# The delta rule's triangular inverse on compact 32x32 diagonal blocks, built by products with its transpose, in place of full 128x128 tiles

## The chip, the cores and the metric

The kernel runs on one NeuronCore of a Trainium2 chip. The metric is the device time of one execution in microseconds (us).

## The reference, cut to what matters

The program is two blocks of two layers each on 256 tokens of width 1024, in fp32: a gated convolution beside a gated DeltaNet, an HGRN2 layer, then a conformer convolution and an attention layer with their MLPs. The change lies in the DeltaNet of the first layer, which has 8 heads of 128 columns. Per head and chunk, with gc the running sum of the gates:

```python
low = jnp.where(strict, jnp.einsum("bhnid,bhnjd->bhnij", kb, k) * decay, 0.0)
rhs = jnp.concatenate([v * beta, kb * jnp.exp(gc)[..., None]], axis=-1)
sol = lax.linalg.triangular_solve(low + jnp.eye(c, dtype=jnp.float32), rhs,
                                  left_side=True, lower=True, unit_diagonal=True)
```

The solution gives the new values of the chunk; with them the state and the outputs are computed. The reference takes chunks of 64 tokens; the kernel takes 128, which is the same function, so that it has two chunks and inverts 128x128 unit triangular matrices.

## The kernel before, in words

Activations lie transposed, 128 channels on the partitions and 256 tokens in a row. A large product is done in halves (`half`, lines 409 to 411): weights are split into a high part (ScalarE, line 542) and a low part (VectorE, line 555) and each of 8 blocks takes three products of 128x128 by 256 columns, 24 instructions. SyncE's queue brings the weights in units of 1 MB into three buffers; some units hold rows of another matrix that VectorE reduces beside the rest (line 547). The order on each engine is written out by hand and engines meet at semaphores.

In the DeltaNet stage the eight heads are two groups of four (g = 0, 1), a matrix of each head in one quarter of a PSUM bank; each group has three banks b0, b1, b2. `weave` runs the groups' generators in turn, a step of group 0, a step of group 1, then one step of the filler: on TensorE one half product of the gated convolution, the output projection or the z gate (`pe_fill`). ScalarE and VectorE have the same order (`ac_group`, `ve_group`, with `ac_fill`, `ve_fill`).

For each chunk c (two), `pe_group` writes the differences of the gates (line 693, a product with 8 rows), k by k and q by k products (lines 698, 702). VectorE forms the decayed matrix DD (line 296, ScalarE takes the exponential at line 1213), LT = DD times k by k (L1848) and its first masked part ML (L1850), AT_ (L1852) and YY = identity less ML (L1854). TensorE transposes ML (line 300, the helper `tr`) and VectorE makes XX of it (L1860) and the next mask (L1862). Then come six levels s = 1 to 6 (LEVELS is 7); XX is the inverse of the diagonal blocks of size 2^s, YY its transpose. A level has two steps with a filler between:

```python
t = pe.matmul(PS[b0][:, blk(m)], ML[:, m, :], XX[:, m, :], start=True, stop=True)
...
t = pe.matmul(PS[b1][:, blk(m)], YY[:, m, :], PP[:, m, :], start=True, stop=True)
```

The first step (line 730) multiplies the masked off-diagonal part by XX; from level 2 on, four transposes of XX (line 300) into b2 stand ahead of it and ScalarE copies them to YY (L1226). ScalarE copies the product to PP (L1228), the second step (line 742) multiplies by YY, and VectorE subtracts it from XX (L1875); it makes the next ML beside (L1871). Level 6 forms the transpose alone (line 746, L1877). With YY the stage goes on to the new values (line 758), the outputs and the state (lines 765, 769). The convolution of the third layer (`pe_taps`, line 929) has products of 32x32 tiles, and `pe_level` (line 865) and `pe_tap_sum` (line 938) other small ones.

GpSimd clears a few buffers and issues side transfers in order (`pool_program`). The constants K come in one transfer: identity, ones, masks `gm` of seven levels, and `quad`, an identity of 32 repeated down the partitions.

## Time and profile before

| what | us |
|---|---|
| median of 3 runs (1408.59 to 1410.61) | 1410.13 |
| the profiled execution | 1410.44 |
| its span | 1408.3 |
| TensorE busy, share of the span | 1348.1, 96% |
| weight loads busy | 1248.9, 89% |
| VectorE busy | 975.4, 69% |
| ScalarE busy | 747.4, 53% |
| GpSimd busy | 22.4, 2% |

The profiled execution is one run of the program; the span goes from its first to its last instruction, and 2.1 us of the run's time lie around it. Busy times are sums over the whole span. A TensorE instruction is recorded from its start to the end of its pipeline, so that successive ones overlap in the record, and the distance of their starts tells what each takes. Line numbers, as L742, are those of the kernel; a helper has one line for all of its callers.

### The profile page before, as it was taken

Reading aid. Unit: us, or ns where it says so; the run is one execution under the profiler, and the core shown is the slowest. Engines: PE = TensorE matmul, PEld = TensorE weight load, DVE = VectorE, ACT = ScalarE, POOL = GpSimd, SP = SyncE. Lnnn points to the kernel's source line nnn. Section 1 sums busy time; section 2 is a strip of 40 time slices with the busy share of each in tenths; the row PEclk is TensorE's granted clock in tenths of the full one; section 3 lists DMA queues with packets and bytes.
Section 4 is the critical chain, followed back from the end, with each engine's and each line's share of the span. In section 5 each row is a group of like instructions: output and inputs, shape, how many; then the busy total and the mean of one; then the engine's idle time right before and its main releaser. Section 6 shows DMA issues by size and latency. Waiting matters only on the chain.

```text
span 1408.3 us, 24667 instructions
## 1 busy us (share of the span) xinstructions
PE 1348.1 (96%) x10464; PEld 1248.9 (89%) x10464; DVE 975.4 (69%) x1491; ACT 747.4 (53%) x989; POOL 22.4 (2%) x53
## 2 busy tenths in 40 slices
PE   6998998999989999999799998899999999999998
PEld 5997998999979999999798776888888998988887
DVE  4887977765466788777644686788776676576543
ACT  6666344437454455555245413778634686487531
POOL 0000000000000000000000000000000000000000
PEclk9998999999999999999899999999999999999999
DMA  6555553444266555555232323568875433355551
GB/s 254 184 194 191 183 215 133 188 168 147 98 224 225 182 202 190 205 209 181 91 120 90 121 91 122 180 222 288 300 269 206 150 120 121 131 185 194 190 195 64
DMA packets 34637, 247.22 MB, mean 176 GB/s; under 512 B 3872, under 2 KB 3872, under 8 KB 4960
## 3 DMA queue, kind: packets, MB, share of 16 engines
q1 hardware_dynamic: 29968, 213.40, 42.2%
q0 software_dynamic: 4560, 32.25, 6.5%
q8 instruction: 83, 1.36, 0.4%
q14 instruction: 26, 0.21, 0.0%
HBM read 244.58 MB, written 1.05 MB: 174 GB/s over the span
## 4 chain that ended last, share of the span: by engine, by line
PE 82%; DVE 8%; ACT 6%; issue 3%; DMA 1%; DVEq 0%; ACTq 0%
PE PS L467 14%; PE PS L409 9%; PE PS L410 9%; PE PS L411 9%; PE PS L468 7%; PE PS L482 6%; PE PS L865 3%; ACT WH L542 3%; DVE WL L555 2%; PE PS L425 2%; PE PS L929 2%; PE PS L426 2%; PE PS L427 2%; PE PS L742 1%; PE PS L730 1%
## 5 line engine op out<-in xcount | busy, mean ns | idle before, releaser
L555 DVE TENSOR_TENSOR WL<-RAW,WH 128x2048 fp32r<-128x2048 f32 x166 | 380.0, 2289 | 118.3 <-ACT WH L542 115.0
L542 ACT ACTIVATE WH<-RAW 128x2048 fp32r<-128x2048 f32 x166 | 317.0, 1910 | 182.2 <-PE PS L468 71.2
L409 PE MATMUL PS<-XW,WH 128*128 128x256 f32 x1024 | 301.1, 294 | 16.8 <-DVE WL L555 12.4
L410 PE MATMUL PS<-XW,WH 128*128 128x256 f32 x1024 | 293.2, 286 | 0.0
L411 PE MATMUL PS<-XW,WL 128*128 128x256 f32 x1024 | 292.9, 286 | 0.0
L409 PEld LDWEIGHTS PS<-XW,WH 128*128 128x128 f32 x1024 | 200.0, 195 | 18.4 <-DVE WL L555 12.4
L410 PEld LDWEIGHTS PS<-XW,WH 128*128 128x128 f32 x1024 | 200.1, 195 | 0.2
L411 PEld LDWEIGHTS PS<-XW,WL 128*128 128x128 f32 x1024 | 199.8, 195 | 0.0
L467 PE MATMUL PS<-XW,WH 128*128 128x512 f32 x392 | 141.0, 398 | 0.2
L296 DVE SCALAR_TENSOR_TENSOR BIG<-BIG,C 128x256 f32<-128x256 f32 (+2 forms) x228 | 101.4, 505 | 30.0 <-ACT BIG L1264 13.5
L468 PE MATMUL PS<-XW,WL 128*128 128x256 f32 x392 | 109.9, 280 | 0.0
L482 PE MATMUL PS<-BIG,RAW 128*128 128x258 f32 (+1 forms) x448 | 102.9, 387 | 2.2 <-issue 2.2
L482 PEld LDWEIGHTS PS<-BIG,RAW 128*128 128x128 f32 x448 | 85.2, 192 | 18.8 <-issue 6.7
L467 PE MATMUL PS<-YW,WH 128*128 128x512 f32 x256 | 90.7, 398 | 0.0
L467 PEld LDWEIGHTS PS<-XW,WH 128*128 128x128 f32 x392 | 73.7, 188 | 16.5 <-DVE WL L555 0.9
L467 PE MATMUL PS<-HX,WH 128*128 128x512 f32 x240 | 85.4, 397 | 0.0
L468 PEld LDWEIGHTS PS<-XW,WL 128*128 128x128 f32 x392 | 74.0, 189 | 2.3
L468 PE MATMUL PS<-YW,WL 128*128 128x256 f32 x256 | 71.9, 281 | 0.0
L547 DVE CUSTOM_DVE_ANT_0 BIG<-BIG,CB 128x1024 f32<-128x1024 f32 x60 | 71.2, 1224 | 0.0
L468 PE MATMUL PS<-HX,WL 128*128 128x256 f32 x240 | 67.5, 281 | 0.0
L409 PE MATMUL PS<-YW,WH 128*128 128x256 f32 x224 | 67.1, 299 | 0.2 <-DVE YW L1788 0.2
L410 PE MATMUL PS<-YW,WH 128*128 128x256 f32 x224 | 65.4, 292 | 0.0
(368 smaller groups left out, 2677.4 us busy)
## 6 DMA issues: line engine op xcount, KB each, us to landing
RAW<-wst SPq DMA_DIRECT2D x200, 1024.0 KB, 4.9
BIG<-wad POOLq DMA_DIRECT2D x30, 1024.0 KB, 5.1
X<-xT SPq DMA_DIRECT2D x1, 1024.0 KB, 4.9
outT<-X SPq DMA_DIRECT2D x4, 256.0 KB, 4.2
K<-cst SPq DMA_DIRECT2D x1, 656.0 KB
CB<-crow SPq DMA_DIRECT2D x1, 512.0 KB
BIG<-pT POOLq DMA_DIRECT2D x2, 256.0 KB, 4.2
C<-cols SPq DMA_DIRECT2D x1, 370.0 KB
```

What stands on the lines that cost most here:

```text
L296: return ve.scalar_tensor_tensor(out=o, in0=a, scalar=s, in1=b, op0=op0, op1=op1)
L409: pe.matmul(o, h, hl[0][:, k0 + k, :], start=(k == 0), stop=False)
L410: pe.matmul(o, h, hl[1][:, k0 + k, :], start=False, stop=False)
L411: t = pe.matmul(o, l, hl[0][:, k0 + k, :], start=False, stop=(k == 7))
L425: pe.matmul(o, h, wh[:, k, :], start=(k == 0), stop=False)
L467: pe.matmul(two(b + n), h, op, start=start, stop=False)
L468: return pe.matmul(PS[b + n][:, 0:T], l, op[:, 0, :], start=False, stop=False)
L482: t = pe.matmul(o, w[:, k, n * 128:(n + 1) * 128], op(k), start=(k == 0), stop=(k == 7))
L542: ac.activation(WH[p % NS][:, :], RAW[u % NR][:, :], ACT.Copy).then_inc(S.hi.tick(p), 1)
L547: t = ve.tensor_tensor_reduce(out=w, in0=w, in1=CB1[:, :], scale=1.0, scalar=0.0, op0=ALU.mult, op1=ALU.add, accum_out=MOD[:, 2 * n + m:2 ...
L555: ve.tensor_tensor(WL[p % NS][:, :], RAW[u % NR][:, :], WH[p % NS][:, :].bitcast(f32), ALU.subtract).then_inc(S.lo.tick(p), 1)
L865: t = pe.matmul(PS[b][:, m * 64:(m + 1) * 64], k[:, m // 2, blk(m % 2)], qs[:, m, :, 1, :], start=True, stop=True)
```

## The change

The inverse of the four diagonal blocks of 32 is kept compact: for each head 128 partitions by 32 columns, block a on partitions 32a to 32a+31. XYB holds X in its first four heads' columns and Y, the transpose, in the other four.

- VectorE makes LTB, the diagonal blocks of LT, in four operations on 32 partitions each, masks them with `gmb` (MLB) and starts Y from `quad`; the first transpose becomes a product of MLB by `quad`.
- Levels 1 to 4: TensorE takes each product as 16 matmuls of 32x32 by 32 columns for a group. It forms both X's and Y's update, 32 matmuls, from the same copy PPB, and VectorE subtracts both in one operation of 128x256. The transposes of XX and the copies to YY go.
- Level 5 joins pairs of blocks: 8 matmuls with LT, then 12, for X and Y. ScalarE copies Y's diagonal blocks into YY (four operations) and writes the negated off-diagonal ones (two); VectorE writes XG, the part of X that level 6 needs.
- Level 6: for each head one matmul with 64 rows and one with 32, then one of 64x64; VectorE writes the last quarter of YY.
- YY is cleared once by GpSimd, one memset per group. The constants lose two masks of 128 columns and gain `gmb` of 160.

The diff, with lines of context and some plain ones left out:

```diff
-CST = [("ident", 128), ("ones", 128), ("neg", 128), ("gm", 896), ("quad", 32)]
+CST = [("ident", 128), ("ones", 128), ("neg", 128), ("gm", 640), ("quad", 32), ("gmb", 160)]
...
+    put("gmb", np.concatenate([np.concatenate([v[32 * c:32 * c + 32, 32 * c:32 * c + 32] for c in range(4)]) for v in lv], 1).astype(np.float32))
...
+        LTB = [view(7168 + 4096 * g, 4, 32) for g in range(2)]
+        MLB = [view(7296 + 4096 * g, 4, 32) for g in range(2)]
+        XYB = [view(7680 + 4096 * g, 8, 32) for g in range(2)]
+        PPB = [view(6144 + 4096 * g, 4, 32) for g in range(2)]
+        XG = [view(6272 + 4096 * g, 4, 32) for g in range(2)]
+        PP6 = [view(6400 + 4096 * g, 4, 64) for g in range(2)]
...
+            for g in range(2):
+                gp.wait_ge(*S.l2.ve(g, 1))
+                gp.memset(CHB[g][4], 0.0).then_inc(S.gdn.gp.tick("zero", g), 1)
...
-                    t = tr(pe, PS[b0][:, blk(m)], ML[:, m, :])
+                    for a in range(4):
+                        r = slice(32 * a, 32 * a + 32)
+                        t = pe.matmul(PS[b0][r, 32 * m:32 * m + 32], MLB[g][r, m, :], K[r, CST0["quad"][0]:CST0["quad"][0] + 32], start=True, stop=True)
...
-                        vacate(pe, b2, "yy", g, c, s)
-                        for m in range(4):
-                            t = tr(pe, PS[b2][:, blk(m)], XX[:, m, :])
-                        t.then_inc(S.gdn.pe.tick("yy", g, c, s), 1)
...
-                    pe.wait_ge(*S.gdn.ve("ml", g, c, s))
+                    pe.wait_ge(*(S.gdn.ve("ml", g, c, s) if s < 5 else S.bank[b1]("kk", g, c)))
...
-                        t = pe.matmul(PS[b0][:, blk(m)], ML[:, m, :], XX[:, m, :], start=True, stop=True)
+                        if s < 5:
+                            for a in range(4):
+                                r = slice(32 * a, 32 * a + 32)
+                                t = pe.matmul(PS[b0][r, 32 * m:32 * m + 32], MLB[g][r, m, :], XB[r, m, :], start=True, stop=True)
+                        elif s == 5:
+                            for a in (0, 64):
+                                r, o = slice(a, a + 32), slice(a + 32, a + 64)
+                                t = pe.matmul(PS[b0][o, 32 * m:32 * m + 32], LT[r, m, o], XB[r, m, :], start=True, stop=True)
+                        else:
+                            pe.matmul(PS[b0][64:128, 64 * m:64 * m + 32], LT[0:64, m, 64:128], XG[g][0:64, m, :], start=True, stop=True)
+                            t = pe.matmul(PS[b0][64:128, 64 * m + 32:64 * m + 64], LT[32:64, m, 64:128], XB[32:64, m, :], start=True, stop=True)
...
-                    if s < 6:
+                    if s < 5:
...
                         for m in range(4):
-                            t = pe.matmul(PS[b1][:, blk(m)], YY[:, m, :], PP[:, m, :], start=True, stop=True)
+                            for a in range(4):
+                                r = slice(32 * a, 32 * a + 32)
+                                pe.matmul(PS[b1][r, 32 * m:32 * m + 32], YB[r, m, :], PPB[g][r, m, :], start=True, stop=True)
+                        for m in range(4):
+                            for a in range(4):
...
+                                t = pe.matmul(PS[b1][r, 128 + 32 * m:160 + 32 * m], PPB[g][r, m, :], YB[r, m, :], start=True, stop=True)
+                    elif s == 5:
...
+                        for m in range(4):
+                            pe.matmul(PS[b1][32:64, 32 * m:32 * m + 32], YB[32:64, m, :], PPB[g][32:64, m, :], start=True, stop=True)
+                            for a in (0, 64):
...
+                                t = pe.matmul(PS[b1][r, 128 + 32 * m:160 + 32 * m], PPB[g][o, m, :], YB[o, m, :], start=True, stop=True)
...
+                        pe.wait_ge(*S.gdn.ac("y5", g, c))
...
                         for m in range(4):
-                            t = pe.matmul(PS[b2][:, blk(m)], PP[:, m, :], YY[:, m, :], start=True, stop=True)
+                            t = pe.matmul(PS[b2][0:64, 64 * m:64 * m + 64], PP6[g][64:128, m, :], YY[64:128, m, 64:128], start=True, stop=True)
...
+                    if s == 6:
+                        ac.wait_ge(*S.gdn.pe("p", g, c, 5))
+                        for a in (64, 0):
+                            t = ac.activation(YY[a:a + 32, :, a + 32:a + 64], PS[b1][a:a + 32, 128:256].rearrange("p (a b) -> p a b", a=4), ACT.Copy, scale=-1.0)
+                        t.then_inc(S.gdn.ac.tick("y5", g, c), 1)
...
-                    if s > 1:
-                        ac.wait_ge(*S.gdn.pe("yy", g, c, s))
-                        ac.activation(YY, grp(b2), ACT.Copy).then_inc(S.bank[b2].tick("yy", g, c, s, on="ac"), 1)
...
-                    ac.activation(PP, grp(b0), ACT.Copy).then_inc(S.bank[b0].tick("pp", g, c, s, on="ac"), 1)
+                    if s < 6:
+                        ac.activation(PPB[g], PS[b0][:, 0:128].rearrange("p (a b) -> p a b", a=4), ACT.Copy).then_inc(S.bank[b0].tick("pp", g, c, s, on="ac"), 1)
+                    else:
+                        ac.activation(PP6[g][64:128, :, :], PS[b0][64:128, 0:256].rearrange("p (a b) -> p a b", a=4), ACT.Copy).then_inc(S.bank[b0].tick("pp", g, c, s, on="ac"), 1)
+                    if s == 5:
+                        ac.wait_ge(*S.bank[b1]("xx", g, c, 4))
+                        if c == 0:
+                            ac.wait_ge(*S.gdn.gp("zero", g))
+                        for a in range(0, 128, 32):
+                            ac.activation(YY[a:a + 32, :, a:a + 32], YB[a:a + 32, :, :], ACT.Copy)
...
+                for a in range(0, 128, 32):
+                    t = ve.tensor_tensor(LTB[g][a:a + 32, :, :], DD[a:a + 32, :, a:a + 32], grp(b1)[a:a + 32, :, a:a + 32], ALU.mult)
+                t.then_inc(S.gdn.ve.tick("ltb", g, c), 1)
+                ve.wait_ge(*own("ve"))
+                ve.tensor_tensor(MLB[g], LTB[g], bm(cs("gmb", 0, 32), 4), ALU.mult).then_inc(S.gdn.ve.tick("ml", g, c, 0), 1)
+                ve.wait_ge(*own("ve"))
+                ve.tensor_tensor(YB, bm(cs("quad", 0, 32), 4), MLB[g], ALU.subtract).then_inc(S.gdn.ve.tick("y0", g, c), 1)
                 ve.tensor_tensor(LT, DD, grp(b1), ALU.mult).then_inc(S.bank[b1].tick("kk", g, c, on="ve"), 1)
-                ve.wait_ge(*own("ve"))
-                ve.tensor_tensor(ML, LT, bm(cs("gm"), 4), ALU.mult).then_inc(S.gdn.ve.tick("ml", g, c, 0), 1)
...
-                ve.wait_ge(*S.gdn.ve("ml", g, c, 0))
-                ve.tensor_tensor(YY, bm(cs("ident"), 4), ML, ALU.subtract).then_inc(S.gdn.ve.tick("y0", g, c), 1)
...
-                ve.tensor_tensor(XX, bm(cs("ident"), 4), grp(b0), ALU.subtract).then_inc(S.bank[b0].tick("x0", g, c, on="ve"), 1)
+                ve.tensor_tensor(XB, bm(cs("quad", 0, 32), 4), small(PS[b0][:, 0:128]), ALU.subtract).then_inc(S.bank[b0].tick("x0", g, c, on="ve"), 1)
...
-                    if s < 6:
+                    if s < 4:
                         ve.wait_ge(*S.gdn.pe("m", g, c, s))
-                        ve.tensor_tensor(ML, LT, bm(cs("gm", 128 * s + 128), 4), ALU.mult).then_inc(S.gdn.ve.tick("ml", g, c, s + 1), 1)
+                        ve.tensor_tensor(MLB[g], LTB[g], bm(cs("gmb", 32 * s + 32, 32), 4), ALU.mult).then_inc(S.gdn.ve.tick("ml", g, c, s + 1), 1)
+                    if s == 5:
+                        ve.wait_ge(*S.bank[b1]("xx", g, c, 4))
+                        ve.tensor_copy(XG[g][0:32, :, :], XB[0:32, :, :])
...
-                    if s < 6:
-                        ve.tensor_tensor(XX, XX, grp(b1), ALU.subtract).then_inc(S.bank[b1].tick("xx", g, c, s, on="ve"), 1)
+                    if s < 5:
+                        ve.tensor_tensor(XYB[g], XYB[g], small(PS[b1][:, 0:256]), ALU.subtract).then_inc(S.bank[b1].tick("xx", g, c, s, on="ve"), 1)
+                    elif s == 5:
+                        ve.wait_ge(*S.gdn.ac("y5", g, c))
+                        ve.tensor_scalar(XG[g][32:64, :, :], small(PS[b1][32:64, 0:128]), -1.0, None, ALU.mult).then_inc(S.bank[b1].tick("xx", g, c, s, on="ve"), 1)
                     else:
-                        ve.tensor_tensor(YY, YY, grp(b2), ALU.subtract).then_inc(S.bank[b2].tick("yq", g, c, on="ve"), 1)
+                        ve.tensor_scalar(YY[0:64, :, 64:128], PS[b2][0:64, 0:256].rearrange("p (a b) -> p a b", a=4), -1.0, None, ALU.mult).then_inc(S.bank[b2].tick("yq", g, c, on="ve"), 1)
```

## Rows read from the trace of the kernel before

**Rows 1.** The page, busy time by engine: us, share, instructions

```profile
PE 1348.1 (96%) x10464; PEld 1248.9 (89%) x10464; DVE 975.4 (69%) x1491; ACT 747.4 (53%) x989; POOL 22.4 (2%) x53
```

**Rows 2.** Stretches of 20 us: busy TensorE, weight loads, VectorE, ScalarE, GpSimd, clock

```profile
130.00:150.00 20.00, 16.24 (x100) 15.54 (x99) 17.33 (x35) 7.98 (x11) 0.00 (x0) 0.75 0.23 82
150.00:170.00 20.00, 20.00 (x172) 19.83 (x173) 16.95 (x26) 6.69 (x11) 0.00 (x0) 1.00 0.58 212
...
230.00:250.00 20.00, 14.16 (x95) 13.53 (x94) 19.09 (x31) 4.49 (x6) 0.00 (x0) 0.83 0.28 106
...
sum 200.00, PE 184.87 PEld 181.11 DVE 155.78 ACT 88.22 POOL 0.00; mean PE 18.49 PEld 18.11 DVE 15.58 ACT 8.82 POOL 0.00
```

**Rows 3.** The chain, 157 to 171 us: start, length, engine, tile, line

```profile
164.28 1.78 PE PS L742 x16
...
168.46 0.12 PE PS L411
...
168.94 0.44 PE PS L300 x4
169.38 0.89 PE PS L730 x8
```

**Rows 4.** TensorE's waits, 130 to 305 us: total, times, longest

```profile
PE PS L300 <- DVE BIG L1850: 7.5, 2, 4.4
PE PS L742 <- ACT BIG L1228: 2.6, 2, 1.5
PE PS L730 <- DVE BIG L1862: 2.0, 2, 1.3
```

**Rows 5.** Groups of instructions, 140 to 305 us: busy us, mean ns, idle

```profile
L555 DVE TENSOR_TENSOR WL<-RAW,WH 128x2048 fp32r<-128x2048 f32 x15 | 34.3, 2287 | 3.6 <-ACT WH L542 3.6
L547 DVE CUSTOM_DVE_ANT_0 RAW<-RAW,CB 128x1024 f32<-128x1024 f32 x28 | 33.1, 1220 | 0.0
...
L742 PE MATMUL PS<-BIG 128*128 128x128 f32 x160 | 19.8, 277 | 2.6 <-ACT BIG L1228 2.6
...
L1228 ACT ACTIVATE BIG<-PS 128x512 f32<-128x512 f32 x24 | 14.5, 604 | 1.0 <-PE PS L730 1.0
...
L1871 DVE TENSOR_TENSOR BIG<-BIG,K 128x512 f32<-128x512 f32 x20 | 13.2, 687 | 4.2 <-PE PS L730 4.2
L1875 DVE TENSOR_TENSOR BIG<-BIG,PS 128x512 f32<-128x512 f32 x20 | 12.8, 682 | 0.0
```

**Rows 6.** The convolution's taps in order of time: start, length, idle before

```profile
795.32 2.28 PEld L929 LDWEIGHTS PS<-BIG 32*32 32x32 f32 x128 [0.33 <-DVE BIG L2207]
...
823.90 0.35 PEld L929 LDWEIGHTS PS<-BIG 32*32 32x32 f32 x33 [0.33 <-issue]
```

**Rows 7.** TensorE in order of time, 222 to 229 us

```profile
222.36 0.28 PE L411 MATMUL PS<-XW,WL 128*128 128x256 f32 x1
222.57 1.15 PE L693 MATMUL PS<-RW,K 8*128 8x128 f32 x8
...
228.52 0.36 PE L409 MATMUL PS<-XW,WH 128*128 128x256 f32 x1
```

**Rows 8.** Groups by form: smaller shapes of VectorE, ScalarE and GpSimd

```profile
L2058 DVE TENSOR_TENSOR BIG<-BIG 128x256 f32<-128x256 f32 x8 | 3.3, 418 | 0.0
...
L2058 DVE TENSOR_TENSOR BIG<-BIG 128x128 f32<-128x128 f32 x8 | 2.3, 285 | 0.0
...
L1425 ACT ACTIVATE BIG<-PS 32x128 f32<-32x128 f32 x8 | 2.1, 269 | 0.1
...
L628 POOL MEMSET BIG<- 128x512 f32 x2 | 1.0, 543 | 0.0
```

**Rows 9.** ScalarE in order of time, 178 to 188 us

```profile
180.03 1.28 ACT L1176 ACT_TABLE_LOAD   x1
...
183.25 1.90 ACT L542 ACTIVATE WH<-RAW 128x2048 fp32r<-128x2048 f32 x1
185.05 0.58 ACT L1226 ACTIVATE BIG<-PS 128x512 f32<-128x512 f32 x1
```

16 lines of the change are left out of this document (11 added, 5 removed).

## The prediction

> **What bounds the kernel now.** I began with the page's busy shares, went to the stretches of 20 us for the stage that is edited, then to its groups of instructions, its waits and its chain. The page shows TensorE busy 96% of the span [rows 1], but that is over stages that differ. In the edited stage, 110 to 310 us, TensorE is busy 184.9 of 200 us, and all of it in a stretch like 150 to 170, VectorE 155.8, ScalarE 88.2 [rows 2]. The chain there runs nearly wholly over TensorE: a piece of filler (24 instructions of 0.12 us, 2.9 in all), then a step of both groups of heads, then filler again [rows 3]. So here TensorE's time in order is the time of the stage, save where it waits. Between 130 and 305 us its waits are few: 7.5 us for the first masked tile (L1850), 2.6 for ScalarE's copies (L1228), 2.0 for L1862 [rows 4]. A step that gets shorter on TensorE is therefore worth its length, as long as VectorE and ScalarE still finish behind the 2.9 us of filler between two steps.
>
> **What is removed.** An fp32 matmul is two load-and-multiply pairs: L742 has 160 records for 80 matmuls [rows 5]. They follow at 1.78/16 = 0.111 us, a transpose at 0.44/4 = 0.11 us [rows 3]. Per chunk, for both groups, level 1 costs 1.78 + 1.78 and each of levels 2 to 6 costs 2 x (0.44 + 0.89) + 1.78 = 4.44, so 25.8 us; the two chunks 51.5. The transposes of the first mask add 2 x 0.88 = 1.8. TensorE gives up **53.3 us**.
>
> **What is added on TensorE.** Let g be the time of 16 matmuls of 32x32x32, four on each diagonal tile, 32 instructions. Levels 1 to 4 need one g for the product with the mask and two for the inverse and its transpose: 3 x 4 levels x 4 (two groups, two chunks) = 48 g. Level 5 has 8 + 12 matmuls, 1.25 x 4 = 5 g; the first transpose, now a product, 4 g. Together 57 g. No row has this shape. The nearest is the convolution's taps, 32x32 tiles but 256 columns and all 16 tiles: 128 loads in 2.28 us, 17 ns each, so g = 0.55; a burst there starts 33 loads within 0.35 us less the last one's 0.10, 8 ns each, so g = 0.25 [rows 6]. A pass now streams 32 columns instead of 256, which speaks for the lower end; only 4 tiles share the load instead of 16, and each gets the next matmul at once, which speaks for the upper. I take 0.42, near the middle, and 57 x 0.42 = 23.9 us. The far bound, no overlap at all, is 32 x 0.111 = 3.6 us a group.
>
> Going from full width to small tiles and back costs time. L693 uses 8 rows; from the first L693 to the filler behind, 222.57 to 228.52, 48 instructions take 5.95 us where 48 x 0.111 = 5.33 would do, and the entry is 0.21 us instead of 0.12 [rows 7]. That is two visits, about **0.35 us a visit**. There is one per step of levels 1 to 5 and per step of level 6, 12 in a chunk, and 2 more in the second chunk, where full-width transposes and products stand between the groups: 26 visits, 9.1 us. The first transpose has 2 + 1, 1.0 us. Level 6 alternates 64-row and 32-row tiles: 16 changes a chunk at half a visit, 0.18, is 2.9; its last product has 16 instructions with half the weight columns, 16 x 0.055 = 0.9. Both chunks: 7.6 us. The sum is 23.9 + 9.1 + 1.0 + 7.6 = 41.6, so TensorE's own part is **-11.7 us**.
>
> **What the other engines give or take.** VectorE: a level loses 687 + 682 ns and gets 285 for a 128x128 mask and 418 for the 256-column update [rows 5, 8]; about 0.67 us a level and group. ScalarE loses two copies of 0.60 and gets one of about 0.28. Both are behind filler in most steps: nothing. Three places count.
> - The wait on L1850 stays, and the chain into it grows. Instead of L1848 + L1850 (1.37) come four quadrant products and the mask, 5 x 0.285 = 1.43; behind them, ahead of the second group, come 0.29 + 0.69 + 0.69 instead of 0.69 + 0.69. So the second group is 0.45 us later, in two chunks: **+0.9**.
> - The wait on L1862: L1860 and L1862 fall from 1.37 to 0.57 a group. Of the 2.0 us of waits [rows 4] I take **-1.5**.
> - The waits on L1228 hang on ScalarE, which comes late from a table load, a SiLU and a 1.9 us weight copy; then L1226 for the transpose, then L1228 [rows 9]. With L1226 gone and L1228 small TensorE goes on 0.8 us earlier; but TensorE alone would have saved 2.66 - 0.35 - 0.84 = 1.5 in the step before. Twice 0.7 is given back: **+1.3**.
> The constants are 96 columns shorter, 48 KB: -0.2 at the start. The two memsets on POOL (0.54 each [rows 8]) stand in its queue ahead of transfers that wait for a much later stage, and are needed only at level 5: nothing; without that cover 1 us. At level 5 ScalarE has four quadrant copies a group, some 0.27 each [rows 8], with the second group's small copy queued behind the first's four, 1.1 us, under 2.9 of filler: nothing. Level 6 gets a wait that was not there: VectorE's XG waits for ScalarE's two negated copies, and TensorE's first product for both. 4 x 0.27 + 0.3 = 1.4 us lies under the same filler; uncovered, it would be up to 1.4 in each chunk. Behind the waiting XG on VectorE stands only work that has a whole filler to spare.
>
> Sum: -11.7 + 0.9 - 1.5 + 1.3 - 0.2 = **-11.2 us**. The profiled execution took 1410.44 us (span 1408.3), the median is 1410.13, 0.3 apart; the forecast is made from the median, **1399**.
>
> **Rivals.**
> 1. *The small matmuls run faster than I take.* For it: the burst of 8 ns. At g = 0.25, 57 x 0.17 = 9.7 us less: 1389.
> 2. *VectorE or ScalarE becomes the bound.* VectorE is busy 15.6 us in 20 on the mean [rows 2] and two groups' updates now follow sooner on weight splits of 2.3 us and side reductions of 2 x 1.2 us [rows 5]. Against it: a level takes more from VectorE (1.3 us for both groups) than from TensorE, where the levels go from 51.5 to 38.9 us (41.6 without the first transposes' 1.0 + 1.7), 1.05 for each of twelve. If each of the 8 levels 2 to 5 waits 1 us more: 1407, no change or barely.
> 3. *Slower: an issue floor or the shared bank.* This is the mechanism on the other side, and its place is the run of 32-instruction groups. The taps write each row of tiles to its own PSUM bank; here the four row groups write one bank. If they take turns, or if an instruction costs a floor however few its columns, g grows. The point from which it decides is g = 0.42 + 11.2/57 = 0.62, 19 ns an instruction, just above the taps' 17. [...]
>
> The rows on starts weigh against the floor: 17 ns on the mean, 8 in a burst. [...]
>
> 4. *The change does not do what it says*, the small tiles being run at full width one after another: g = 3.6, +180 us. The taps' rows show that the chip does run 32x32 tiles beside each other, so I leave 0.01.
>
> TensorE's clock: the granted share is 0.75 in 130 to 150 us and 0.83 in 230 to 250 [rows 2], stretches in which it waited for L1850. Those waits stay. [...] Should there be one more like that at 230, it costs 20 x 0.17 = 3.4 us; I keep that within the range.
>
> **Chances.** The forecast's own case, g from 0.33 to 0.55 (1393.9 to 1406.4), 0.45; rival 1, 0.20; rival 2, 0.16, of which 0.13 within the bound below and 0.03 faster; rival 3, 0.18; rival 4, 0.01. A measurement of this kernel tells about 0.2%, 2.8 us, from no change. Faster: 0.45 + 0.20 + 0.03 = 0.68; within: 0.13; slower: 0.19. The range reaches from rival 1's 1389 to 1413 (g = 0.67); beyond it lie g under 0.25 and the worse half of rival 3 and all of 4.
>
> **What would show it.** Right: between two fillers of levels 2 to 4, the mask step falls from 2.7 us to about 1.3 and the inverse step stays near 2.0 (0.35 + 4 x 0.42 against 1.8); instructions in a 32x32 block start 13 ns apart; the waits on L1850's successor stay at 7 to 9 us, those on L1862's shrink. Wrong in size: the 32x32 pitch is under 9 or over 19 ns. Wrong in kind: TensorE's waits for ScalarE or VectorE in levels 2 to 6 grow by more than 5 us, the last product of level 5 waits for the next step's quadrant copies, or the clock shows new stretches at 0.5.

## The result, and the profile after

The kernel after takes **1394.08 us** (median; 1390.31 to 1401.87, 4 runs) against 1409.36 of the kernel before beside it (1407.55 to 1410.61, 4 runs): ratio 0.9893, interval 0.9861 to 0.9924. A second set on another chip gave 1396.85 against 1410.83, ratio 0.991 (0.989 to 0.993). Faster by 0.9 to 1.1%. The forecast was 1399 in 1389 to 1413; its time and its sign held. Two of its terms did not, and it is luck that they cancel: that is what the rest of this text is about.

The page of the kernel after, its span and the busy times [rows 1], and its line for the queue that brings the program (before: 83 packets, 1.36 MB):

```profile
span 1388.4 us, 27551 instructions
...
PE 1319.2 (95%) x11904; PEld 1217.3 (88%) x11904; DVE 958.3 (69%) x1503; ACT 737.9 (53%) x993; POOL 23.4 (2%) x55
...
q8 instruction: 94, 1.54, 0.4%
```

The profiled execution took 1390.31 us. TensorE is busy for 29 us less than before but the span is only 19.9 us shorter, so some busy time became waiting. The same stretches as [rows 2], in the order us, busy TensorE, weight loads, VectorE, ScalarE, GpSimd, granted clock:

```profile
130.00:150.00 20.00, 13.10 (x165) 12.18 (x167) 17.12 (x43) 6.36 (x10) 0.00 (x0) 0.74 0.16 54
150.00:170.00 20.00, 20.00 (x600) 19.13 (x587) 17.27 (x31) 7.45 (x12) 0.00 (x0) 1.00 0.70 261
230.00:250.00 20.00, 14.88 (x367) 14.02 (x368) 16.15 (x31) 4.56 (x6) 0.00 (x0) 0.91 0.56 210
```

Between 150 and 170 us TensorE is still never idle: the levels stay bound by it. What one level costs is in TensorE's order of time there (start, length; L743 is the product with the mask, L764 the inverse's, L768 its transpose's, L417 to L419 the filler):

```profile
157.66 0.28 PE L419 MATMUL PS<-XW,WL 128*128 128x256 f32 x1
157.87 0.75 PE L743 MATMUL PS<-BIG 32*32 32x32 f32 x64
158.56 0.38 PE L417 MATMUL PS<-XW,WH 128*128 128x256 f32 x1
158.78 0.28 PE L418 MATMUL PS<-XW,WH 128*128 128x256 f32 x1
...
161.41 0.28 PE L419 MATMUL PS<-XW,WL 128*128 128x256 f32 x1
161.62 0.45 PE L764 MATMUL PS<-BIG 32*32 32x32 f32 x32
161.90 0.48 PE L768 MATMUL PS<-BIG 32*32 32x32 f32 x32
...
163.12 0.28 PE L418 MATMUL PS<-XW,WH 128*128 128x256 f32 x1
```

The mask step takes 158.78 - 157.66 less the two fillers of 0.12 that lie in it: 0.88 us, where it was 2 x (0.44 + 0.89) = 2.66 [rows 3]. The inverse step takes 163.12 - 161.41 - 0.24 = 1.47, where it was 1.78. A level falls by **2.1 us** on TensorE. As in the prediction, an instruction is one multiply of TensorE together with its weight load, so that a 32x32 product in fp32 has two. The two steps hold two and four groups of 16 matmuls and one visit to the small tiles each, so 2g + v = 0.88 and 4g + v = 1.47: g = 0.295 and v = 0.29. The times of single instructions of the new shapes, by groups of 140 to 305 us (busy us, mean ns of one, idle before):

```profile
L768 PE MATMUL PS<-BIG 32*32 32x32 f32 x512 | 8.1, 194 | 1.1 <-issue 1.1
L764 PE MATMUL PS<-BIG 32*32 32x32 f32 x512 | 7.7, 193 | 4.7 <-ACT BIG L1265 2.7 <-issue 2.0
...
L1930 DVE TENSOR_TENSOR BIG<-BIG,PS 128x256 f32<-128x256 f32 x16 | 6.0, 413 | 0.0
...
L1898 DVE TENSOR_TENSOR BIG<-BIG,PS 32x128 f32<-32x128 f32 x12 | 3.4, 284 | 2.8 <-ACT BIG L1247 2.7
```

And TensorE's waits, 130 to 305 us, against [rows 4]:

```profile
PE PS L722 <- DVE BIG L1901: 9.6, 3, 5.1
PE PS L764 <- ACT BIG L1265: 2.7, 2, 2.5
PE PS L743 <- DVE BIG L1914: 2.4, 1, 2.4
PE PS L301 <- DVE BIG L1906: 2.4, 2, 1.3
PE PS L764 <- issue: 2.0, 2, 1.5
PE PS L417 <- DVE YW L1833: 2.0, 1, 2.0
PE PS L768 <- issue: 1.1, 1, 1.1
PE PS L418 <- issue: 1.0, 1, 1.0
PE PS L743 <- issue: 0.6, 1, 0.6
```

L722 is the product that stands for the first transposes, and its wait is the old one on the first masked tile (7.5, now 9.6). New are L301 (keys and values transposed, waiting for the bank of the attention tile, L1906), the filler's L417, and 4.7 us under "issue", that is with nothing that the profile shows to wait for.

The table has, for every profile of this study, the edited stage from the first matmul of L705 (L693 before) to the last product with the state; TensorE's waits within it; what of them is "issue"; the rest; and how long the granted clock was 0.50 between 110 and 320 us. All in us.

| kernel | stage | waits | "issue" | rest | at clock 0.50 |
|---|---|---|---|---|---|
| before | 194.0 | 13.5 | 0 | 180.5 | 20.5 |
| before, again (e1) | 195.5 | 14.9 | 0 | 180.6 | 20.5 |
| after | 184.1 | 25.4 | 4.7 | 158.7 | 17.1 |
| after, again (e2) | 187.0 | 21.8 | 2.9 | 165.2 | 34.1 |
| e3 level 6 grouped | 181.8 | 22.2 | 5.4 | 159.6 | 20.5 |
| e4 after, 16 more | 186.3 | 21.2 | 4.4 | 165.1 | 30.7 |
| e5 before, 16 more | 194.0 | 18.0 | 0 | 176.0 | 10.2 |
| e6 tile by tile | 197.5 | 14.1 | 0 | 183.4 | 34.1 |
| e7 VectorE's order | 180.8 | 25.2 | 7.2 | 155.6 | 13.7 |
| e8 one copy more | 187.7 | 20.6 | 5.4 | 167.1 | 37.5 |
| e9 full width, both | 207.9 | 18.4 | 0 | 189.5 | 20.5 |
| e10 e7, 32 more | 176.1 | 18.4 | 3.5 | 157.7 | 20.5 |
| e11 after, 48 more | 184.8 | 19.0 | 0 | 165.8 | 30.7 |
| e12 after, 32 more | 180.6 | 20.5 | 2.4 | 160.1 | 20.5 |

So the stage gained 10.0 us in the first pair and 8.6 in the second: TensorE's own part fell by 21.8 (by 15.4 in the second, where 13.7 us more at clock 0.50 cost up to 6.8, if all that ran in them took twice its time; the filler's multiplies start 0.213 us apart in such a stretch, 144.2 to 145.9 us of before, and 0.12 at clock 1.00), and 7 to 12 us of it came back as waits. The two profiles of after differ by 2.9 us in the stage with the same program, so stage lengths of single profiles settle nothing under some 3 us. The median gained 15.3 and 14.0. Most of what is missing lies behind the stage, and is the subject of the next section too.

### The profile page after: what moved, and what is told of

It is laid out like the page before. It is cut to its first block, busy times and chain, and to the rows that moved or that the text cites. A ratio compares the mean times of both kernels' runs of the same rounds, so it can differ in the third digit from the quotient of the medians.

```text
span 1388.4 us, 27551 instructions
## 1 busy us (share of the span) xinstructions
PE 1319.2 (95%) x11904; PEld 1217.3 (88%) x11904; DVE 958.3 (69%) x1503; ACT 737.9 (53%) x993; POOL 23.4 (2%) x55
## 4 chain that ended last, share of the span: by engine, by line
PE 82%; DVE 8%; ACT 6%; issue 3%; DMA 1%; DVEq 0%; ACTq 0%
PE PS L475 14%; PE PS L417 10%; PE PS L418 9%; PE PS L419 9%; PE PS L476 7%; PE PS L490 6%; PE PS L899 3%; ACT WH L550 3%; DVE WL L563 2%; PE PS L433 2%; PE PS L435 2%; PE PS L434 2%; PE PS L963 2%; PE PS L456 1%; PE PS L457 1%
## 5 line engine op out<-in xcount | busy, mean ns | idle before, releaser
L417 PE MATMUL PS<-XW,WH 128*128 128x256 f32 x1024 | 301.6, 295 | 16.6 <-DVE WL L563 12.3
L419 PE MATMUL PS<-XW,WL 128*128 128x256 f32 x1024 | 293.2, 286 | 0.0
L417 PEld LDWEIGHTS PS<-XW,WH 128*128 128x128 f32 x1024 | 200.4, 196 | 19.0 <-DVE WL L563 12.3
L419 PEld LDWEIGHTS PS<-XW,WL 128*128 128x128 f32 x1024 | 199.7, 195 | 1.1 <-issue 1.1
L297 DVE SCALAR_TENSOR_TENSOR BIG<-BIG,C 128x256 f32<-128x256 f32 (+2 forms) x228 | 101.3, 504 | 29.9 <-ACT BIG L1309 13.5
L417 PE MATMUL PS<-YW,WH 128*128 128x256 f32 x224 | 66.7, 298 | 2.0 <-DVE YW L1833 2.0
```

Source lines behind the costliest of these rows:

```text
L297: return ve.scalar_tensor_tensor(out=o, in0=a, scalar=s, in1=b, op0=op0, op1=op1)
L417: pe.matmul(o, h, hl[0][:, k0 + k, :], start=(k == 0), stop=False)
L419: t = pe.matmul(o, l, hl[0][:, k0 + k, :], start=False, stop=(k == 7))
```

## The experiments

My theories at this point: **T**, the small products are cheap because four tiles of TensorE work side by side; **W**, the levels are bound by TensorE's own work, not by the chain through VectorE and ScalarE (**C**, the rival); **F**, the "issue" waits are TensorE's program arriving late, so they follow the count of instructions and not the work. The expectations e1 and e2 use letters of their own: their **A** puts the part of the gain that lies behind the stage down to the clock, their **B** to later stages that are really quicker. What e1, e5 and e11 call 1.2 GHz is in the profiles a granted clock of 0.50; no profile gives the clock in GHz. The block of 256 instructions that the expectations on F count with was my estimate, and no row shows it. What is shown: 83 and 94 transfers of 16 KB on q8 for TensorE's 20928 and 23808 instructions (multiplies and loads), 252 and 253 for each.

**The two kernels again (e1, e2).**

> The kernel before, unchanged, profiled a second time. Two theories on why the changed kernel's span is 20.0 us shorter while the edited stage is only 9.5 + 0.5 us shorter. Theory A (clock windows): the other 10 us come from stretches at 1.2 GHz that fell otherwise behind the stage; then this second profile differs from the first by some us behind 340 us and by under 0.5 us within 120 to 320, and the ratio to the kernel before is 1.000 +- 0.003. Theory B (the later stages are really quicker behind the edit): this profile agrees with the first within 1 us everywhere.

> The changed kernel, unchanged, profiled a second time. Theory A (clock windows): the stage is again 10 us shorter than before, the rest differs from the first profile by several us; ratio about 0.991 (10 us for the stage and 2 to 5 for the rest). Theory B: again 20 us shorter, with the same 10 us behind the stage, ratio 0.986. Both theories expect the stage's waits on issue (4.7 us in the first profile, all at the small products of the second chunk) at the same instructions if they hang on how many instructions TensorE has read since the program's start, and elsewhere if they are chance.

Measured: 1412.09 us, ratio 1.0005 (0.9988 to 1.0021), and 1396.85, ratio 0.991 (0.989 to 0.993). The second pair repeats the first, with a larger part of the stage at clock 0.50 in the profile of after (34.1 us instead of 17.1). The ratio is the one of A. But B is right for one place: 4.2 us behind the stage stand in both pairs alike (see e5). The waits on "issue" were to come at the same instructions if they hang on the count, and they do. With TensorE's multiplies counted from the program's start, the five in the first profile's second chunk come when 2620, 2747, 2874, 3000 and 3381 have been started, the five in the second profile's at 2747, 2874, 3000, 3127 and 3381. Their lengths differ (0.2 to 1.5 us). The distances are 126 or 127 multiplies or multiples of that.

**Level 6 grouped by shape (e3).** The matmuls of 64 rows and of 32 rows of L749 and L750 no longer alternate:

```
                         else:
                             pe.matmul(PS[b0][64:128, 64 * m:64 * m + 32], LT[0:64, m, 64:128], XG[g][0:64, m, :], ...)
-                            t = pe.matmul(PS[b0][64:128, 64 * m + 32:64 * m + 64], LT[32:64, m, 64:128], XB[32:64, m, :], ...)
+                    if s == 6:
+                        for m in range(4):
+                            t = pe.matmul(PS[b0][64:128, 64 * m + 32:64 * m + 64], LT[32:64, m, 64:128], XB[32:64, m, :], ...)
```

> Level 6's first products in another order: for each group first the four with 64 rows, then the four with 32, so 4 changes of tile shape in a step of both groups instead of 16. Theory (a change of shape costs time each): in the changed kernel such matmuls of two instructions start 0.23 us apart, of which 0.15 is the change; 12 fewer changes save 12 x about 0.12 = 1.5 us a chunk, 3 us in all, ratio to the changed kernel 0.998. Rival (64-wide weight loads and the two dependent passes set the 0.23): under 0.5 us in all, no difference that can be measured.

Measured: 1392.22 us, ratio 0.9875 (0.9854 to 0.9896). TensorE in order of time (start, length) in the first chunk, the kernel after:

```profile
192.60 0.30 PE L749 MATMUL PS<-BIG 64*64 64x32 f32 x2
192.83 0.30 PE L750 MATMUL PS<-BIG 32*64 32x32 f32 x2
...
196.01 0.42 PE L750 MATMUL PS<-BIG 32*64 32x32 f32 x2
...
200.75 1.14 PE L780 MATMUL PS<-BIG 64*64 64x64 f32 x16
```

and the version with the shapes apart:

```profile
193.80 0.65 PE L749 MATMUL PS<-BIG 64*64 64x32 f32 x8
194.38 0.65 PE L752 MATMUL PS<-BIG 32*64 32x32 f32 x8
```

Sixteen pieces of two instructions start 0.228 us apart, 3.6 us in all. Four pieces of eight start 0.58 apart, 2.3 us in all. Per piece c + 2i = 0.228 and c + 8i = 0.58 give i = 0.059 an instruction and c = 0.11 for the change of shape. Twelve changes less in a chunk are 1.3 us, in both chunks **2.6 us**. The median is 4.6 us under e2's, the intervals overlap.

**One tile at a time (e6).** The loops over heads and tiles are exchanged at levels 0 to 4; for the product with the mask and for the inverse:

```
                         if s < 5:
-                            for a in range(4):
-                                r = slice(32 * a, 32 * a + 32)
-                                t = pe.matmul(PS[b0][r, 32 * m:32 * m + 32], MLB[g][r, m, :], XB[r, m, :], ...)
+                            for a in range(4):
+                                r = slice(32 * m, 32 * m + 32)
+                                t = pe.matmul(PS[b0][r, 32 * a:32 * a + 32], MLB[g][r, a, :], XB[r, a, :], ...)
...
-                        for m in range(4):
-                            for a in range(4):
+                        for a in range(4):
+                            for m in range(4):
                                 r = slice(32 * a, 32 * a + 32)
                                 pe.matmul(PS[b1][r, 32 * m:32 * m + 32], YB[r, m, :], PPB[g][r, m, :], ...)
```

> The kernel after with the loops of the small products at levels 0 to 4 exchanged: all four heads of one 32x32 tile of TensorE first, then the next tile, instead of the four tiles in turn. The same products, the same instructions. Theory T: a tile is busy for some 34 ns with one instruction of 32 columns, and the 9 ns between instructions that the profile shows come of four tiles working side by side. Then 32 instructions of a group of 16 products take from 0.28 us up to about 1.1 us, unless the engine looks past a waiting instruction; 57 groups would give up to +40 us, ratio up to 1.03. If the engine can hold a few instructions per tile and go on, the cost lies between: 0.5 us per group, ratio 1.005 to 1.01. Rival: instructions are sent at 9 ns whatever tile they go to: no change, ratio 1.000 against the kernel after (0.989 to 0.991 against before).

Measured: 1406.45 us, ratio 0.9957 (0.9944 to 0.9970). TensorE in order of time, at a granted clock of 1.00:

```profile
159.81 1.51 PE L743 MATMUL PS<-BIG 32*32 32x32 f32 x64
...
164.31 0.80 PE L764 MATMUL PS<-BIG 32*32 32x32 f32 x29
```

The first of these rows is the same 64 instructions as the row of 157.87 above. Take off the last one's 0.19 and divide by 63: 21 ns from one start to the next, where four tiles in turn give (0.75 - 0.19)/63 = 8.9 ns. So T holds, in its middle form: the speed of the small products comes of taking the four tiles in turn, and 16 matmuls tile by tile take 0.67 us instead of 0.29. The 34 ns of a tile were an estimate (four times the 0.28 us of a group, over its 32 instructions); the row shows 21. For the 52 groups of levels 0 to 4 that is 19.8 us; the table's "rest" shows 18.2 more than e2's, with the same time at clock 0.50. But the stage grew by 10.5 only: waits fell from 21.8 to 14.1, and the "issue" ones among them to 0. More than two fifths of the slowing was taken out of waits. That is a hint that a part of the waits in the kernel after is room that fast products have opened, not a cost by itself.

**One more copy on the chain (e8).**

```
                     if s < 6:
+                        ac.activation(PP6[g][0:64, :, 0:32], PS[b0][0:64, 0:128].rearrange("p (a b) -> p a b", a=4), ACT.Copy)
                         ac.activation(PPB[g], PS[b0][:, 0:128].rearrange("p (a b) -> p a b", a=4), ACT.Copy).then_inc(...)
```

> The kernel after with one more ScalarE copy of the same size (128 columns, 64 partitions, into a place that nobody reads) ahead of each copy of the masked product at levels 1 to 5: 20 copies of about 0.27 us, each one between a product and the product that waits for it. Theory C: the small products left TensorE short of cover, so that the stage is partly bound by the chain through VectorE and ScalarE; a part of the 5.4 us shows: +2 to +5 us, ratio 0.992 to 0.994. Rival (the engine bound by TensorE's own work, as in my prediction's sum): the copies lie beside the projection's products that fill the wait, +0 to +0.5 us, ratio 0.990.

Measured: 1395.99 us, ratio 0.9885 (0.9871 to 0.9900), against 0.991 and 0.9893 of the kernel after. Of the 5.4 us (the 20 copies take 5.2 in the trace, 261 ns each) nothing shows; I had given 0.992 to 0.994 for the other case, which lies outside. TensorE's wait for ScalarE's copy didn't grow either (0.2 us at L764, against 2.7 and 2.5 in the two profiles of the kernel after). The levels have that much slack behind the filler: W stands, C falls for the path through ScalarE. VectorE's part of the levels was not lengthened and isn't tested.

**VectorE's order (e7), on the version of e3.** The attention tile and the full masked tile go ahead of the start value of Y:

```
                 ve.tensor_tensor(MLB[g], LTB[g], bm(cs("gmb", 0, 32), 4), ALU.mult)...
-                ve.wait_ge(*own("ve"))
-                ve.tensor_tensor(YB, bm(cs("quad", 0, 32), 4), MLB[g], ALU.subtract)...
-                ve.tensor_tensor(LT, DD, grp(b1), ALU.mult)...
                 ve.wait_ge(*S.gdn.pe("qk", g, c))
                 ve.tensor_tensor(AT_, DD, grp(b2), ALU.mult)...
+                ve.tensor_tensor(LT, DD, grp(b1), ALU.mult)...
+                ve.wait_ge(*S.gdn.ve("ml", g, c, 0))
+                ve.tensor_tensor(YB, bm(cs("quad", 0, 32), 4), MLB[g], ALU.subtract)...
```

> The version with the last level's two shapes kept apart (ratio 0.9875 before), in which VectorE makes the attention tile and the full masked tile (lines 1904 to 1906 of the kernel after) ahead of the compact start value of the transpose instead of behind it. Theory C: the key and value transposes of TensorE (line 301 of the kernel after) wait 2.4 us in total for the attention tile, and nobody waits for the start value until the first product pair: the wait falls by some 0.28 us at each of four places, the stage by 0.5 to 1 us, ratio 0.987. Rival: the wait is taken over by the next one in the chain (the first masked compact tile has to be there for the x0 product anyway): no change within 0.3 us.

Measured: 1392.91 us, ratio 0.9863 (0.9850 to 0.9876); e3 had 0.9875. Its wait at L301:

```profile
PE PS L301 <- DVE BIG L1906: 1.5, 2, 0.9
```

In the kernel after the two waits there are 1.28 and 1.08 us, here 0.86 and 0.67, so each is 0.4 us shorter. But e3's own profile has only one of them (1.3), and its TensorE waited for the first masked tile twice and not three times (L722: 7.2 us, here 9.2). And the stage, 1.0 us shorter than e3's, had 6.8 us less at clock 0.50. So a gain of 0.5 to 1 us in the stage is not shown, and the times can't tell the two versions apart. The first part of the chain, to the first masked tile, is untouched.

**Full width, both by products (e9).** The second half of the change without the first, in the kernel before:

```
-                        vacate(pe, b2, "yy", g, c, s)
-                        for m in range(4):
-                            t = tr(pe, PS[b2][:, blk(m)], XX[:, m, :])
...
                             pe.matmul(PS[b1][:, blk(m)], YY[:, m, :], PP[:, m, :], ...)
+                        vacate(pe, b2, "yy", g, c, s)
+                        for m in range(4):
+                            t = pe.matmul(PS[b2][:, blk(m)], PP[:, m, :], YY[:, m, :], ...)
...
-                        ac.activation(YY, grp(b2), ACT.Copy)...
...
+                        ve.tensor_tensor(YY, YY, grp(b2), ALU.subtract)...
```

> The kernel before, full 128 columns wide as it was, but with the transpose of the inverse carried along by products: at levels 1 to 5 the four transposes of X and ScalarE's copy of them (0.44 and 0.60 us in the profile of before) are gone, and there are instead four products of PP and Y (0.89 us) and VectorE's update of Y (0.69 us). It is the second half of the change without the first. Theory W (TensorE's own work sets the stage): 20 x (0.89 - 0.44) = +9.0 us of TensorE, ratio 1.006; with VectorE's 20 x 0.69 = 13.8 us, on an engine that is busy for 156 us of the 200 of the stage, up to 1.010. The gain of the change is then of the small tiles alone, by more than its whole size. Rival: what the change brings comes of the shorter chain of a level (one trip from product to copy to product less), and the full width hardly matters: ratio 1.000 or below.

Measured: 1418.57 us, ratio **1.0063** (1.0050 to 1.0075). TensorE's waits in the stage:

```profile
PE PS L300 <- DVE BIG L1848: 8.6, 3, 4.4
PE PS L726 <- DVE BIG L1860: 5.0, 3, 2.3
PE PS L740 <- ACT BIG L1226: 2.5, 2, 1.9
```

In the table the rest grows from 180.5 to 189.5, the 9.0 us that 20 x (0.89 - 0.44) gives, with the same time at clock 0.50, and the waits by 3.5 to 5 (the row of L726 is the one that was 2.0 [rows 4]). Behind the stage the execution gave 4 us back, as the next experiment explains. Carrying the transpose by products is no gain by itself: at full width it costs. It pays because it lets four 32x32 tiles stand for the whole, where a product costs 0.29 instead of 0.89.

**Where the program is cut (e4, e5, e11, e12).** In the second chunk of the kernel after, each "issue" wait ends 2.2 to 2.5 us after the start of a 16 KB transfer on the program's queue (q8; the transfer itself takes 0.9 to 1.0 us):

```profile
244.01 0.29 PE L764 MATMUL PS<-BIG 32*32 32x32 f32 x13 [1.51 <-issue]
248.93 0.27 PE L743 MATMUL PS<-BIG 32*32 32x32 f32 x9 [0.64 <-issue]
253.72 0.21 PE L764 MATMUL PS<-BIG 32*32 32x32 f32 x1 [0.48 <-issue]
259.61 0.28 PE L418 MATMUL PS<-XW,WH 128*128 128x256 f32 x1 [0.97 <-issue]
275.25 0.26 PE L768 MATMUL PS<-BIG 32*32 32x32 f32 x7 [1.13 <-issue]
```

The transfers begin at 241.8, 246.6, 251.5, 257.4 and 272.8. By count the waits are 127 multiplies apart, with as many loads. (A wait of 0.2 to 0.3 us that every profile has between 1064 and 1098 us follows no transfer; I leave it out.) A multiply of the small products follows at 9 ns, so 127 of them pass in 1.1 us, half of the 2.2 to 2.5 us from a transfer's start to the end of the wait; 127 of the filler's take 15 us. To move the cuts and nothing else I added n unused 32x32 products ahead of the second chunk:

```
                 vacate(pe, b0, "row", g, c)
+                if c and g == 0:
+                    for q in range(n):
+                        r = slice(32 * (q % 4), 32 * (q % 4) + 32)
+                        pe.matmul(PS[b0][r, 0:32], K[r, quad], K[r, quad], start=True, stop=True)
```

with n = 16 in the kernel after (e4):

> 16 more 32x32 matmuls (64 TensorE instructions) are put ahead of the second chunk's first products; their results are overwritten. They cost 0.3 us themselves. Theory F (instruction fetch: TensorE reads its program in blocks of 256 instructions, and waits when a dense step uses up a block before the next is there): the waits on issue in the second chunk, 4.7 us in all at six places, move to other instructions and change in size, to anything from 1 to 7 us. Rival (the waits on issue belong to these steps, whatever the block): they stand at the same lines and levels with the same lengths, and the kernel is 0.3 us slower.

and n = 16 in the kernel before (e5):

> The kernel before with 16 unused 32x32 products added once, behind the release of the second chunk's row bank (64 TensorE instructions in the count of matmuls and weight loads together; the same addition that shifted the kernel after by 16 products). Its work in the stage grows by some 0.5 us. Theory F: the 2.25 us that the kernel before waits for nothing else at line 482 (808.28 in its profile, with a 1.2 GHz stretch right behind it) is a piece of TensorE's program that comes late, and where in the program it falls is a matter of how many instructions stand before it; the kernel after has 2880 more, which is 11 x 256 + 64. So 64 more put the kernel before in the place of the kernel after: the wait at 482 goes from 2.2 to at most 0.9, the gap to the kernel after behind the stage shrinks by 2 to 4 us, and the ratio is 0.997 to 0.999. Rival: the 4.3 us behind the stage come from something else that the change left there (shorter mask constants, the memsets of GpSimd, other start times of transfers): the wait at 482 stays 2.2 and the ratio is 1.000 to 1.001.

In e4 the waits stand at other lines, and the time is the same (1395.07, ratio 0.9899, 0.9876 to 0.9923). By count they stand where they stood, at 2621, 2748, 3001 and 3254: the cuts stay and the work moves past them, as F says.

```profile
244.96 0.32 PE L772 MATMUL PS<-BIG 32*32 32x32 f32 x15 [0.71 <-issue]
249.91 0.59 PE L747 MATMUL PS<-BIG 32*32 32x32 f32 x40 [0.66 <-issue]
258.97 0.44 PE L747 MATMUL PS<-BIG 32*32 32x32 f32 x27 [0.61 <-issue]
269.52 0.43 PE L747 MATMUL PS<-BIG 32*32 32x32 f32 x14 [2.05 <-issue]
```

e5 gave 1407.91 us, ratio **0.9961** (0.9946 to 0.9976): the kernel before, with work added, is 0.4% faster, somewhat more than the 0.997 to 0.999 that I had given to F, and outside the rival's 1.000 to 1.001. TensorE in order of time in the stage of the taps, first before:

```profile
802.23 3.39 PE L929 MATMUL PS<-BIG 32*32 32x256 f32 x160
805.55 0.48 PE L482 MATMUL PS<-BIG,RAW 128*128 128x256 f32 x1
808.28 5.19 PE L482 MATMUL PS<-BIG,RAW 128*128 128x256 f32 x15 [2.25 <-issue]
816.03 3.72 PE L482 MATMUL PS<-BIG,RAW 128*128 128x256 f32 x16
```

and e5:

```profile
806.69 3.72 PE L482 MATMUL PS<-BIG,RAW 128*128 128x256 f32 x16
812.97 3.72 PE L482 MATMUL PS<-BIG,RAW 128*128 128x256 f32 x16
```

Before, TensorE has just run 160 multiplies of the taps, 21 ns each, and one of full width; then it stands for 2.25 us until 2.2 us after a transfer's start (806.12), and the granted clock is 0.50 for 3.4 us from 809.2 on, 0.9 us behind the wait's end (the 15 instructions take 5.19 us instead of some 3.5). In e5 both are gone: the 16 that start at 816.03 before start at 812.97, although the taps' first sum came 1.1 us later (802.80 against 801.66). From that sum to the first sum of squares it is 61.7 and 61.8 us in the two profiles of before, and 57.5 to 57.8 us in all twelve other profiles, those of the kernel after among them. So **4.2 us** of the change's gain come of where TensorE's program is cut, and 64 unused instructions give them to the kernel before as well; they have nothing to do with the triangular solve. F holds for this place.

A second wait of this kind lies in the last burst of the taps (3.05 us at 872.27 before, 2.56 at 855.70 after). It is there in all profiles but e11's, in which TensorE waits 3.02 us for ScalarE at that place instead.

e11, n = 48 in the kernel after, was to bring the first of the two waits back:

> The kernel after with 48 unused 32x32 products (192 TensorE instructions, some 0.9 us) ahead of the second chunk. With the 64 by which the change had moved what comes later, this makes 256, so that from there on the program is cut into blocks as it was in the kernel before. Theory F: the wait for the program in the tap stage (2.2 us at line 482 in the kernel before) is back, at its counterpart, with a 1.2 GHz stretch behind it: +2 to +4 us and 0.9 of its own, ratio 0.992 to 0.994. Rival: the wait was tied to something else that the change moved: none comes back, ratio 0.990.

Measured: 1395.53 us, ratio 0.9895 (0.9876 to 0.9913), where I had given 0.992 to 0.994 to F. The interval in the taps' stage is 57.8 us, so the wait did not return as such. The trace shows why:

```profile
797.95 4.06 PE L490 MATMUL PS<-BIG,RAW 128*128 128x256 f32 x16
```

The transfer begins at 798.50, 0.55 us behind the start of this group, much as before (806.12 against 805.55). But the cut lies ten multiplies further on in the same group of 16: TensorE pauses at a count of 7643, and without the change's 1440 and the 96 added that is 6107, where the kernel before stood at 6097. It has ten full-width multiplies to run while the transfer comes, pauses for about 0.3 us and goes on 2.2 us after the transfer's start; the 16 take 4.06 us instead of 3.72. So my arithmetic that 64 + 192 makes a whole block was wrong by ten multiplies, and no run shows where the ten come from. F holds here as well: with the cut at 6097 the wait was 2.25 us, with the cut at what counts as 6107 about 0.3.

What the program's waits cost in the edited stage stays open. e11 has none there, and no other wait grew in their place:

```profile
PE PS L726 <- DVE BIG L1905: 8.0, 3, 4.1
PE PS L768 <- ACT BIG L1269: 2.8, 2, 2.5
```

The first row was 9.6 and 8.9 us in the two profiles of the kernel after, the second 2.7 and 2.5. Its stage is 0.7 us longer than that of the first of these profiles, which had 13.6 us less at clock 0.50, and 2.2 shorter than that of the second, which had 3.4 more. The medians show no gain, but they can't tell less than some 3 us.

**The fastest version (e10),** e7 with n = 32, and n = 32 in the kernel after alone (e12):

> The version with the last level's shapes kept apart and VectorE's order changed (ratio 0.9863 before), with 32 unused 32x32 products (128 TensorE instructions, some 0.6 us) ahead of the second chunk. Theory F: half a block of 256 instructions on, the waits for the program in the second chunk (7.2 us in the profile without them) fall at other instructions, some of them inside the projection's products, where 256 instructions last 15 us instead of 2.3, and cost less there: their sum between 3 and 7 us, and line 482's counterpart gets no wait longer than 1.5 us. Ratio 0.984 to 0.989. Rival: the waits have nothing to do with where a block ends: the same lines and times, ratio 0.987.

> The kernel after with 32 unused 32x32 products (128 TensorE instructions, some 0.6 us of work) ahead of the second chunk: the same shift that stood with the changed order of VectorE and the grouped last level in the run at 0.9833, now alone. Theory F: where the program's blocks end is worth some microseconds by itself, and this shift is a good one: the waits for the program in the stage fall to 0 to 3.5 us from the 2.9 to 4.7 of the two profiles of the kernel after, and in spite of the 0.6 us of added work the time is 1 to 4 us below that of the kernel after: ratio 0.986 to 0.989. Rival: the last 4 us of the 0.9833 came from something that the three edits do only together, or from luck with the clock: ratio 0.990 to 0.991.

e10 gave **1385.85 us**, ratio 0.9833 (0.9819 to 0.9846), the fastest of the study and faster than both kernels, and just below the 0.984 that I had given as the least. Its "issue" waits are 3.5 instead of 7.2, and all of the 3.5 lie in the first chunk, ahead of the added products; in the second chunk e10 and e12 have none, as e11 has none. e12 gave 1395.68, ratio 0.9891 (0.9872 to 0.9911): the shift alone brings the kernel after nothing that can be measured, so that expectation failed. What lies between e7's 0.9863 and e10's 0.9833 isn't settled: the intervals don't touch, so some of it is real, but the two ran on different chips, and the same shift did nothing for the kernel after. It may be worth more where the last level is grouped; no run parts the two. Level 6 grouped is worth 2.6 us by the rows; the order of VectorE nothing that is shown; the rest of e10's lead over the kernel after I leave open.

## Why the prediction was right, and where it was not

**The bound: right.** TensorE's own time sets the levels. The stretch 150 to 170 us has no idle time, a ScalarE copy more in each level costs nothing (e8), and full-width products cost what they take on TensorE (e9, 9.0 us forecast from [rows 3], 9.0 shown).

**What TensorE gives up, 53.3 us: kept.** Nothing contradicts it.

**g = 0.42: too high, the step that failed most.** It is 0.295, 9.2 ns an instruction; 57 x 0.125 = 7.1 us more gain. It lies between rival 1's 0.25 and 0.33, the lower end of the forecast's own case. I took a middle value between the taps' 17 ns and 8 ns [rows 6]; the row of 33 loads in 0.35 us, the burst, was the right neighbour. What I held against it, that only four tiles share the work, matters, since tile by tile an instruction costs 21 ns (e6), but four in turn are enough. Rival 3 falls with it: the four row groups write one PSUM bank and start 9 ns apart, far under the 19 ns from which it would have decided.

**A visit at 0.35: 0.29.** 26 x 0.06 = 1.6 us more gain.

**Level 5 and level 6: a little too low a cost.** The level 6 product takes 16 x 0.228 = 3.6 us in a chunk instead of 2.9, since I counted the changes of shape and left out what lies between them; its last product was right at 0.9 (16 instructions in 1.14 less the last one's length). Level 5 has fewer tiles side by side: the product's 32 instructions take 0.50 to 0.58 us and the inverse's 48 take 0.51, where g = 0.295 would make 0.30 and 0.44 of them. Together some 2 us less gain.

So TensorE's own part should have been -11.7 - 7.1 - 1.6 + 2 = -18.4 by these steps; the table shows -21.8 with 3.4 us less at clock 0.50, which is worth up to 1.7 (half of the 3.4), so -20.1; the second pair, put right in the same way, -22.2. Two to four microseconds remain that I can't assign.

**The waits, +0.7 net: wrong by 6 to 11 us.** They grew by 11.9 and 6.9. This is the second step that failed. Of the single terms, the longer chain to the first masked tile was there (+2.1 instead of +0.9). The -1.5 for L1862 and the +1.3 for L1228 should both be read in L764's 2.7 and L743's 2.4: together 5.1 where 4.6 was (L1228's successor 0.1 more instead of 1.3, L1862's 0.4 more instead of 1.5 less), so neither the gain nor the loss came as I put it. Three were not in my list:
- the transposes of keys and values wait for the bank of the attention tile, which VectorE now makes two operations later behind the first masked tile, after Y's start value and LT (2.4). I had followed the instructions behind the first masked tile only to the second group, not to who waits for the others;
- the filler's own wait for VectorE's YW (2.0, before 0.2);
- the program itself (4.7 and 2.9). The cost of 2880 more instructions, 11 transfers of 16 KB, wasn't in the sum at all.
In part they are less an addition than the other side of the faster products: e6 slows TensorE by 18.2 us and takes 7.7 us out of the waits. What TensorE no longer does in a stage whose delays stay (the first mask 7.5 and 9.6 us, the copies late behind a weight split 2.6 and 2.7) it partly waits for.

**The sum, -11.2: the stage gave -10.0 and -8.6**, because g's error and the waits' error are of nearly one size. That is luck, and it makes the forecast of 1399 look better than its parts. The 4.2 us in the taps' stage, which the forecast didn't have, make up most of the way from there to the -15.3 and -14.0 of the medians. The -0.2 for the shorter constants was an estimate: the page of before moves 254 GB/s in the first fortieth of its span, at which 48 KB take 0.2 us. The remaining 1 to 2 us lie in the long stages around. Their length differs from profile to profile by more than that: from the stage's end to the taps' first sum it is 484.3 and 483.0 before, 482.5 and 481.9 after, and 480.7 to 486.2 over all profiles; behind the taps' stage it is 545.0 and 546.4 before, 540.5 and 544.6 after, and 540.5 to 547.8 over all. So I can't assign them. Had I known g alone, I would have said 1392, and the missing term of the waits would have been covered by the one in the taps' stage.

**Rival 1** (g = 0.25, 1389) is the mechanism that came true in kind, **rival 2** is half of what took it back: not VectorE's or ScalarE's throughput, but delays of theirs that did not shrink (the first masked tile 7.5 us before and 9.6 after, ScalarE's copies 2.6 and 2.7). **Rival 4** is out.

**The signs that I had named.** The mask step fell to 0.88 us instead of 1.3 and the inverse step to 1.47 instead of 2.0; the pitch is 8.9 ns instead of 13, just under the 9 at which I had called the forecast wrong in size. The wait for the first masked tile is 9.6 and 8.9 us, where 7 to 9 was named, and L1862's successor did not shrink. Of the signs for wrong in kind, the waits for ScalarE and VectorE in levels 2 to 6 did not grow by 5 us. New time at clock 0.50 came only in the second pair: 17.1 us against 20.5 in the first, 34.1 against 20.5 in the second, whose median gained 1.3 us less.

## What to carry to other kernels

Count the time a small matmul takes from the nearest burst in which several tiles of the array are active (here 8 ns in the burst, 8.9 in the new products; the mean of the taps was 17), keep consecutive instructions on different tiles (9 against 21 ns), and group equal shapes (0.11 us for each change). When TensorE became much faster in this stage, 6.9 to 11.9 us of some 20 came back as waits, at the places whose delay did not shrink, the program's arrival among them (4.7 and 2.9 us): look for those first. Before a few microseconds far from an edit are put down to it, shift the program by some unused instructions: here that alone moved the old kernel by 0.4% (e5).

## What the runs showed of the hardware

- Four 32x32 tiles in one PSUM bank, fp32: 8.9 ns from one multiply (with its load) to the next (after, 157.87 us), 21 ns when four products in a row go to the same tile (e6, 159.81 us), 16 to 19 ns with two tiles in turn (level 5's product in after, 32 in 0.50 to 0.58 us).
- In the kernel after a step to small tiles and back cost 0.29 us, a change between 64-row and 32-row tiles 0.11 us (after and e3).
- The program came in transfers of 16 KB, one for about 127 multiplies with their loads (94 of them in the kernel after, 83 before). A wait for one ended 2.2 to 2.8 us after the transfer's start, and kernels with the same program up to there have their waits at the same counts of multiplies (2747 in five profiles). These waits stand as "issue" among and right behind the levels' multiplies at 9 ns, and behind 160 of the taps' at 21 ns (2.25 us, with 3.4 us at a granted clock of 0.50 from 0.9 us later on). With the cut ten full-width multiplies further on, 2.25 us became about 0.3 (e11).
- 16 unused products added to the kernel before made it faster: ratio 0.9961, 0.9946 to 0.9976 (e5).
